# A hybrid decoder layer on one core: output projection with the activations in the array and 512 weight columns moving, and three changes of order

## The chip, the core and the metric

The kernel runs on one core of a Trainium2 chip. A core has TensorE (a 128x128 array, fed by weight loads, writing to PSUM), VectorE, ScalarE, GpSimd and SyncE (SP, which here only issues DMAs), each with its own instruction stream, and 16 DMA engines. The streams meet in semaphores that the program waits on by hand. The metric is the time of one execution in microseconds; lower is better.

## What is computed

One layer for 512 prompt rows and 32 sample rows (8 sequences of 4 tokens), model width 2048, fp32 throughout. Cut to what the change touches:

```python
def _prompt_attention(...):       # 4 blocks of 128 queries
    scores = sum_h w[t,h] * relu(qi[t,h] . ki[s])   # 16 index heads of width 64
    _, idx = lax.top_k(causal scores, 128)          # then sparse attention over idx, 8 heads x 128
def _sample_attention(...):       # the same over 1024 cached keys in 8 pages and the new ones, top 256
    ...
def _combine(x, a, p, ga, gb, w_out, ln_g, ln_b):
    mixed = concat([a * silu(ga), p * silu(gb)])    # 2048 wide
    h = 2 ** 0.25 * x + mixed @ w_out               # w_out 2048 x 2048
    y = (h - mean(h)) * rsqrt(var(h) + 1e-5) * ln_g + ln_b
```

## The kernel before

**Three products.** A large product is done in a split format: each fp32 operand becomes a high part (`actH`, `wH`, format fp32r, one pass) and a low part (`actL`, `wL`), and TensorE adds high x high, low x high and high x low. ScalarE makes `wH` from the raw weights (`high`, L656), GpSimd subtracts it from them to get `wL` (`low`, L634). Weights come through four slots of 8 chunks x 128 columns, 512 KB each (`rawW`, loaded by SP at L426). A slot is loaded anew when its `wL` is done (`stage_ready`), and its high part is made anew when its matmuls are done.

**Projections.** `unit` (L1125) multiplies one slot: weights of 128 columns are in the array, 544 activation columns move in two halves of 272, 48 matmuls a unit, two units a tile (L1138). Tile A are the index queries (8 tiles), C the heads, B the pooling mixer, D the output projection (16 tiles). Since D gives outputs by channel, ScalarE copies each tile to `raw`, TensorE turns it back by token (`rows`, L1647 and L1650), and VectorE adds the residual (L2120, L2124), takes the statistics (L2131) and applies the gain (L2137). The first tile of D (`first_tile`, L1483) is interleaved with the last value pages (L1525), chunk by chunk as `actL` gets ready. After the last tile come variance, square root, and the shift vector of each token, which is turned (L1668) and multiplied with `ln_g` and `ln_b` (`correction`, L1677) before VectorE writes y in pieces (L2185) and SP sends it.

**Index tiles.** For each of the 8 tiles of A, TensorE does half a tile, then index products of the tile before (`products`, L1196), then the other half. ScalarE rectifies each product (`rectify`, L713), VectorE adds it to the scores (`add_head`, L1745). The six products of one tile are numbered 0 to 5. ScalarE copies the projected tile to `raw` (L722) after rectifying product 3, VectorE rotates it (`rotate`, L1714 to L1719) after adding product 3, and `qi_ready` tells TensorE that the products with it may start. For the first tile, all six run at once with a zeroed `raw` as operand, waiting only for `qi_ready` 1.

**Softmax of the first heads.** VectorE picks the top 128 of each prompt row eight at a time (`pick_prompt`, L1789 and L1793), between rotations of keys and queries (`rotated`). The order in the first pair is: 2 picks, gate, 3 picks, rotate, 3 picks, rotate, 1 pick, rotate the second key (`rotated(2, ...)`), 2 picks, keep mask (L1863), softmax (L1876).

**Key pages.** When the prompt heads are done, VectorE turns the sample scores into a mask (L1933), ScalarE sends it to memory (`dropD`, L960), VectorE clears `U` and `qPad`, waits for that DMA, clears `probS` (L1939), places the queries (L1944) and copies key page groups from PSUM (`key_copied`, L1951, even ones; ScalarE does the odd ones after copying a tile of B). TensorE turns the keys (L1438) and multiplies them (L1454: four matmuls with 32 columns of the array each). SP spreads the mask back into `probS` (L507).

**SP's order at the end.** In the last group SP interleaves the loads of the first four units of the second and third D tile with the value pages (`unit`, L523). Then it waits for the last attention output, issues the loads of y (L601, 4 MB, and L602), the broadcast gain, waits for VectorE to clear `gb` (L2113, itself after all of y has landed), sends eight rows to `gb` (L608), and goes on with the weights of D.

Of the kernel before, what the change touches and what calls it, by code (L numbers as in the profile page):

```python
# [32 lines left out]
P = 128  # L33
# [37 lines left out]
TILE_A, TILE_C, TILE_B, TILE_D = 1, 9, 41, 57  # L71
SWAP_I = [*range(8, 16), *range(8), *range(16, 32)]
# [89 lines left out]
def layer_program(nc, x_prompt, x_sample, cache_k, cache_v, cache_kidx, state_pool, page_table,  # L162
# [4 lines left out]
    with ctx:  # L167
# [63 lines left out]
        with ExitStack() as s:  # L231
# [29 lines left out]
            def key_slot(n):  # L261

                if n // 2 % 2:
                    return mixed[:, KC - 2 + n % 2, 0:4 * P]
                return kPT[:, n % 2, :, :].rearrange("p h k -> p (h k)")
        with ExitStack() as s:
            y = sb("y", [P, 5, D], F32, s)
            bn = sb("bn", [P, 5, KC, 6], F32, s)
# [5 lines left out]
        gbc = mixed[:].rearrange("p k t -> p (k t)")[:, 0:D]  # L274
# [5 lines left out]
        bank[OUT], bank[SIDE] = acc[0][:, 0, :], acc[0][:, 1, :]  # L280
        dropD = nc.dram_tensor("dropD", [NS, L], F32, kind="Internal").ap()
# [61 lines left out]
        corr_full = sems("corr_full", 2)  # L343
        y_ready = sems("y_ready", 2)
# [57 lines left out]
        yb = banks.stage(["yp0", "ys0", "yp1", "ys1"], four, 8)  # L402
        tb = banks.stage(["t0", "t1", "t2", "t3"], four)
# [5 lines left out]
        def stand_alone(eng):  # L409


            eng.sem_inc(apart, 1)

# [7 lines left out]
        def _(sp):  # L421
# [100 lines left out]

            def unit(j, last=False, g=None):  # L523
# [4 lines left out]
                if last and tile >= 4:  # L528
                    load_unit(wo_view, 1 - half, (tile - 4) * P, t)
# [42 lines left out]
            def group(g, last):  # L572
# [10 lines left out]
                for m in range(PAGES):  # L583
                    if m % 2 == 0:
# [10 lines left out]
            group(LOOPS, True)  # L595

# [7 lines left out]
            sp.dma_start(gbc, ln_g[0].partition_broadcast(P)).then_inc(ln_in, 16)  # L604
# [4 lines left out]
            with sp.Fori(0, 6) as i:  # L609
                for j in range(2):  # L610
                    load_tile(wo_view, (2 * i + 4 + j) * P, TILE_D + 4 + j, i, 2)
            for t in range(TT + 1):
                n = P if t < TT else NS
                dst = y_prompt[0, t * P:(t + 1) * P, :] if t < TT else y_sample.rearrange("b t d -> (b t) d")
                for half in range(2):
                    cols = slice(1024 * half, 1024 * (half + 1))
                    sp.wait_ge(y_ready[t % 2], (t // 2) * (4 if t % 2 else 2) + (half + 1) * (2 if t % 2 else 1))
# [28 lines left out]
        def _(act):  # L646
# [161 lines left out]
            def heads(i, last):  # L808
# [150 lines left out]
            act.wait_ge(drop_ready, 1)  # L959
            act.dma_start(dropD, scoreS[:]).then_inc(drop_out, 16)  # L960


# [27 lines left out]
            copy_tile(0)  # L990
            for m in range(8):
                key_copied("a", m)
            exps(0)
# [100 lines left out]
            with act.Fori(0, 7) as i:  # L1094
                for j in range(2):
                    high(TILE_D + j + 2, 0, i, 2)
                    src, copied = projected(TILE_D + j, i, 2)
                    act.activation(halves(raw[:, j]), src, ACT.Copy).then_inc(copied, 1)
                    high(TILE_D + j + 2, 1, i, 2)
            for j in range(2):  # L1100
                src, copied = projected(TILE_D + 14 + j)
                act.activation(halves(raw[:, j]), src, ACT.Copy).then_inc(copied, 1)
            act.wait_ge(var_ready, 1)
            act.activation(std[:, 0:2], mv[:, 0:2, 1], ACT.Sqrt).then_inc(std_ready, 1)

            b = tb("t0")
            out_of(b, shiftT[:, 0:2 * P], bank_wait(act, b)[:, 0:2 * P])
            act.wait_ge(var_ready, 3)
            act.activation(std[:, 2:5], mv[:, 2:5, 1], ACT.Sqrt).then_inc(std_ready, 1)
            b = tb("t1")  # L1110
            out_of(b, shiftT[:, 2 * P:T], bank_wait(act, b)[:, 0:T - 2 * P])
# [3 lines left out]
        def _(pe):  # L1115
# [83 lines left out]
            for tile in range(H):  # L1199
# [5 lines left out]

                unit(TILE_A + tile, 0)
                if tile == 0:
# [4 lines left out]
                    products(0, 6)  # L1212
                    continue
# [474 lines left out]
            for n in (2, 3):  # L1688
                take(tb(f"t{n}"))
# [565 lines left out]
```

## Time and profile before

| | us |
|---|---|
| median of 3 runs | 1218.41 (1217.15 to 1219.67) |
| the profiled execution | 1214.59 |
| its span, on which all rows stand | 1212.5 |
| TensorE busy | 1179.9 (97%) |
| weight loads busy | 1087.3 (90%) |
| VectorE busy | 597.2 (49%) |
| ScalarE busy | 359.0 (30%) |
| GpSimd busy | 354.1 (29%) |

The profile is one execution. PE is TensorE's matmuls, PEld its weight loads, DVE VectorE, ACT ScalarE, POOL GpSimd, SPq and ACTq DMA issues of SP and ScalarE. A matmul of fp32 operands appears as two instructions. Busy time of overlapping instructions is counted once, so a busy TensorE is not one at its peak.

### The profile page before, as it was taken

The numbers are of one execution on the slowest core, as the hardware profiler recorded it, in microseconds if no ns is written. First come the engines' busy times: TensorE is split into PE (matmuls) and PEld (weight loads), VectorE is DVE, ScalarE is ACT, GpSimd is POOL, SyncE is SP. The second block draws the span as 40 slices with busy tenths as digits, with TensorE's granted clock in tenths as the row PEclk, the third lists the DMA queues.
The fourth block names the chain that finished last, engine by engine and source line by source line (L and its number), as shares of the span: only waits on it lengthen the run. The fifth ranks groups of instructions, "written<-read, shape, count | busy, mean of one in ns | idle before, by whom it ended". The sixth has DMA issues, their size and how long they took to land.

```text
span 1212.5 us, 26754 instructions
## 1 busy us (share of the span) xinstructions
PE 1179.9 (97%) x10300; PEld 1087.3 (90%) x10300; DVE 597.2 (49%) x1083; ACT 359.0 (30%) x665; POOL 354.1 (29%) x150
## 2 busy tenths in 40 slices
PE   6999999999999999999989999999999999999995
PEld 6888889999999999999987889888889879999992
DVE  3666658874665657451444622623523552323226
ACT  4333333223323323322333322322323342122210
POOL 2432222333333334334311311311321223333310
PEclk9999999999999999999999999999999999999996
DMA  7543143233232223354226857857867656222203
GB/s 250 130 121 80 48 111 89 70 88 89 79 104 82 80 79 98 93 154 129 62 85 196 287 208 245 300 194 250 287 207 248 214 189 219 82 76 86 69 1 147
DMA packets 197975, 170.50 MB, mean 141 GB/s; under 512 B 19890, under 2 KB 178538, under 8 KB 196658
## 3 DMA queue, kind: packets, MB, share of 16 engines
q1 hardware_dynamic: 184458, 160.48, 42.7%
q10 hardware_dynamic: 13424, 8.67, 2.4%
q8 instruction: 72, 1.18, 0.4%
q14 instruction: 21, 0.17, 0.0%
HBM read 159.47 MB, written 9.74 MB: 140 GB/s over the span
## 4 chain that ended last, share of the span: by engine, by line
PE 91%; DVE 6%; issue 1%; DMA 1%; ACT 1%; DVEq 0%; SPq 0%; ACTq 0%
PE acc L1138 67%; PE bank L1438 5%; PE bank L1454 3%; PE acc L1525 3%; PE bank L1196 2%; PE bank L1332 2%; PE bank L1313 2%; DVE scoreP L1793 1%; PE acc L1579 1%; DVE top L1789 1%; PE acc L1483 1%; DMA xnat<-in_x_prompt 1%; PE bank L1248 1%; DVE y L2185 1%; PE bank L1322 1%
## 5 line engine op out<-in xcount | busy, mean ns | idle before, releaser
L634 POOL TENSOR_TENSOR wL<-rawW,wH 128x1024 fp32r<-128x1024 f32 (+1 forms) x146 | 353.9, 2425 | 811.4 <-ACT wH L656 811.4
L1138 PE MATMUL acc<-actH,wH 128*128 128x272 f32 (+1 forms) x2304 | 491.5, 294 | 1.2 <-DVE actL L1707 1.2
L1138 PE MATMUL acc<-actH,wL 128*128 128x272 f32 (+1 forms) x2304 | 476.6, 288 | 0.0
L1138 PE MATMUL acc<-actL,wH 128*128 128x272 f32 (+1 forms) x2304 | 475.0, 288 | 0.0
L1138 PEld LDWEIGHTS acc<-actH,wH 128*128 128x128 f32 (+1 forms) x2304 | 360.1, 188 | 23.9 <-issue 21.9
L1138 PEld LDWEIGHTS acc<-actL,wH 128*128 128x128 f32 (+1 forms) x2304 | 361.4, 188 | 0.0
L1138 PEld LDWEIGHTS acc<-actH,wL 128*128 128x128 f32 (+1 forms) x2304 | 359.1, 188 | 0.0
L656 ACT ACTIVATE wH<-rawW 128x1024 fp32r<-128x1024 f32 (+1 forms) x146 | 153.7, 1054 | 226.2 <-PE acc L1138 210.3
L2120 DVE SCALAR_TENSOR_TENSOR y<-y,bank 128x512 f32 (+1 forms) x16 | 11.0, 688 | 122.3 <-PE bank L1647 120.4
L1438 PE MATMUL bank<-sq,kPage 128*128 128x128 f32 x480 | 65.6, 280 | 4.1 <-DVE kPT L1951 4.0
L1438 PEld LDWEIGHTS bank<-sq,kPage 128*128 128x128 f32 x480 | 52.9, 142 | 14.5 <-issue 9.8
L1951 DVE COPY mixed<-bank 128x512 f32<-128x512 f32 x32 | 22.1, 692 | 86.9 <-PE bank L1438 86.5
L1745 DVE SCALAR_TENSOR_TENSOR scoreP<-relu,wiN,scoreP 128x256 f32<-128x256 f32 (+2 forms) x54 | 45.6, 885 | 33.4 <-ACT relu L713 33.4
L1891 DVE SCALAR_TENSOR_TENSOR mixed<-bank,gate 128x128 f32<-128x128 f32 x32 | 9.3, 292 | 82.2 <-PE bank L1332 82.2
L670 ACT ACTIVATE kPT<-bank 128x512 f32<-128x512 f32 x32 | 19.1, 598 | 92.1 <-PE bank L1438 92.1
L713 ACT ACTIVATE relu<-bank 128x512 f32<-128x512 f32 (+3 forms) x63 | 28.9, 502 | 56.4 <-PE bank L1196 33.0
L670 ACT ACTIVATE mixed<-bank 128x512 f32<-128x512 f32 x32 | 19.1, 598 | 85.6 <-PE bank L1438 79.6
L1830 DVE MAX8 top<-scoreS 32x8 f32<-32x1056 f32 x32 | 39.9, 1247 | 3.1
L1951 DVE COPY kPT<-bank 128x512 f32<-128x512 f32 x32 | 22.1, 691 | 39.0 <-PE bank L1438 38.3
L1525 PE MATMUL acc<-vPage,probST 128*4 128x128 f32 x1024 | 39.5, 273 | 0.0
L1833 DVE MATCH_REPLACE8 scoreS<-top,scoreS 32x1056 f32<-32x1056 f32 x32 | 39.4, 1230 | 0.0
L1525 PEld LDWEIGHTS acc<-vPage,probST 128*4 128x4 f32 x1024 | 26.6, 87 | 13.3 <-issue 1.5
(207 smaller groups left out, 1019.6 us busy)
## 6 DMA issues: line engine op xcount, KB each, us to landing
rawW<-in_w_in SPq DMA_DIRECT2D x112, 512.0 KB, 3.8
vPage<-in_cache_v SPq DMA_DIRECT2D x64, 512.0 KB, 4.8
kPage<-in_cache_k SPq DMA_DIRECT2D x60, 512.0 KB, 4.6
rawW<-in_w_out SPq DMA_DIRECT2D x32, 512.0 KB, 4.1
y<-in_x_prompt SPq DMA_DIRECT2D x4, 1024.0 KB, 9.3
out_y_prompt<-y SPq DMA_DIRECT2D x8, 512.0 KB, 2.8
xnat<-in_x_prompt SPq DMA_DIRECT2D x2, 1024.0 KB, 7.9
xnat<-in_x_prompt ACTq DMA_DIRECT2D x2, 1024.0 KB, 10.9
```

Source lines behind the costliest of these rows:

```text
L634: pool.tensor_tensor(wL[:, slot, :, 0:width], rawW[:, slot, :, 0:width], wH[:, slot, :, 0:width].bitcast(F32), ALU.subtract).then_inc(stag ...
L656: act.activation(wH[:, t.slot, :, 0:width], rawW[:, t.slot, :, 0:width], ACT.Copy).then_inc(high_ready[t.slot], 1)
L670: act.activation(dst, src, ACT.Copy).then_inc(bank_free[b.slot], 1)
L713: act.activation(relu[0:rows, t.slot, 0:n], src[0:rows, 0:n], ACT.Relu).then_inc(relu_full[t.slot], 1)
L1138: last = pe.matmul(acc[t.slot][0:width, e, 0:HT], w[:, u.slot, k, 0:width], a[:, kk, e * HT:(e + 1) * HT], start=(half == 0 and k == 0 and ...
L1438: last = pe.transpose(dst[:, (2 * e + a) * P:(2 * e + a + 1) * P], page[:, h * P:(h + 1) * P], ident)
L1454: last = pe.matmul(bank[st.slot][j * SPAN:(j + 1) * SPAN, pair % 2 * 256:pair % 2 * 256 + 256], qPad[:, x % 2, h * NS:(h + 1) * NS], keys, ...
L1525: return pe.matmul(bank[o.slot][j * SPAN:j * SPAN + NT, a * P:(a + 1) * P], probs, values, start=start and a == 0, stop=stop and a == HALF ...
L1745: dve.scalar_tensor_tensor(sc, relu[:, r.slot, 0:(t + 1) * P], wiN[:, t - 1, ds(h, 1)], sc, ALU.mult, ALU.add).then_inc(bank_free[b.slot], 1)
L1830: own.step(dve.max(top, scores))
L1833: own.step(dve.match_replace(scores, top, scores, PICKED))
L1951: dve.tensor_copy(key_slot(2 * m), bank_wait(dve, b)[:]).then_inc(bank_free[b.slot], 1)
```

## The change

**Output projection.** The activations are in the array (128 tokens at a time) and 512 weight columns move. The outputs come by token, and the copies and turning back go. There are four blocks of 512 output columns, and 8 units of two chunks x 512 columns in each; a unit is one slot of 512 KB. `out_tiles` multiplies a unit with the four prompt tiles, 24 matmuls. The 32 sample rows are done with fp32 weights and activations from the raw slots: after each pair of units, four matmuls of 32 array columns each (`sample_parts`), one for each of the pair's four chunks, accumulate in four groups of 32 partitions; at the end of a block ScalarE copies them out and one matmul with a folding matrix adds the four groups (`folded`). Five PSUM banks are used for each block, in a ring of eight. Because the raw weights are read by TensorE, a slot is loaded anew only when its pair is done (`pair_done`), and the units 4 to 7 of the first block are loaded after the last group's other loads, waiting for pairs 1 and 2. In the last block the first two token tiles are finished ahead of the others. Statistics, gain, square root, correction and output go one token tile at a time, the sample tile third.

**Index tile.** Of the first tile's six products, three run as before, and three after the first half of the next tile.

**Softmax.** `rotated(2, ...)` moves behind the last two picks.

**Key pages.** The mask is made and sent after the last softmax, ahead of the last gating; key page group 0 is copied ahead of the clearing; `probS` is cleared before `qPad` and `U`; the first key groups use the other pair of buffers; ScalarE copies two key groups before the tile of B.

```diff
+WIDE = 4 * P
+BLOCKS = D // WIDE
+PAIRS = (4, 5, 6, 7, 0, 1, 2, 3)
+NORMED = (0, 1, TT, 2, 3)
...
-                if n // 2 % 2:
+                if n // 2 % 2 == 0:
                     return mixed[:, KC - 2 + n % 2, 0:4 * P]
...
+            def load_out_unit(t, n, col, done):
+                if done is None:
+                    sp.wait_ge(stage_ready[t.slot], t.free)
+                else:
+                    sp.wait_ge(pair_done, done)
...
-                    load_unit(wo_view, 1 - half, (tile - 4) * P, t)
+                    load_out_unit(t, j - 8, 0, None if j < 12 else (j - 12) // 2 + 1)
...
-                    if m % 2 == 0:
+                    if m % 2 == 0 and not last:
                         unit(12 + m // 2, last, g)
...
             group(LOOPS, True)
+            for j in range(12, 16):
+                unit(j, True, LOOPS)
...
-            with sp.Fori(0, 6) as i:
-                for j in range(2):
-                    load_tile(wo_view, (2 * i + 4 + j) * P, TILE_D + 4 + j, i, 2)
-            for t in range(TT + 1):
+            with sp.Fori(0, BLOCKS - 1) as i:
+                for n in range(8):
+                    load_out_unit(turn(2 * TILE_D + 8 + n, 4, i, 8), n, (i + 1) * WIDE, 4 * i + (n + 4) // 2 + 1)
...
                     exps(1)
+                    act.wait_ge(drop_ready, 1)
+                    act.dma_start(dropD, scoreS[:]).then_inc(drop_out, 16)
                     probs_turned(1, range(TT))
...
-                    products(0, 6)
+                    products(0, 3)
                     continue
+                if tile == 1:
+                    products_of(0, 3, 6)
                 pe.wait_ge(qi_ready, tile + 1)
...
+            def rows_times(q, t, n, first=False, last=False):
+                for c in range(2):
+                    k = 2 * PAIRS[n % 8] + c
+                    for w, parts in ((wH, (actH, actL)), (wL, (actH,))):
+                        for a in parts:
+                            end = pe.matmul(out_bank(q), a[:, k, t * P:(t + 1) * P], wide(w, n, c),
+                                            start=first and c == 0 and w is wH and a is actH,
+                                            stop=last and c == 1 and w is wL)
...
+            def sample_parts(p):
+                q = 5 * (p // 4) + TT
+                weights_ready(2 * p + 1)
...
+                for j in range(4):
+                    n, c = 2 * p + j // 2, j % 2
+                    end = pe.matmul(out_bank(q)[NS * j:NS * (j + 1), :], mixed[:, 2 * PAIRS[n % 8] + c, NP_:T], wide(rawW, n, c),
+                                    start=p % 4 == 0, stop=p % 4 == 3, skip_group_check=True)
+                end.then_inc(pair_done, 1)
...
+            for n in range(4, 8 * BLOCKS - 4):
+                out_tiles(n)
+                if n % 2:
+                    sample_parts(n // 2)
+                if n % 8 == 0:
+                    folded(n // 8 - 1)
...
+            weights_ready(a)
+            weights_ready(b)
+            sample_parts(4 * BLOCKS - 2)
+            for t in range(2):
+                rows_times(first + t, t, a)
+                rows_times(first + t, t, b)
+            weights_ready(c)
+            rows_times(first, 0, c)
+            weights_ready(d)
+            rows_times(first, 0, d, last=True)
+            sample_parts(4 * BLOCKS - 1)
...
-            picks(1)
+            picks(TOPK_P // ROUND - len(EARLY) - 8)
             rotated(2, kT, 1, 0)
-            picks(TOPK_P // ROUND - len(EARLY) - 9)
...
+            normal(0)
+            normal(1)
+            normal(2)
+            finished(0)
+            normal(3)
+            finished(1)
+            finished(2)
+            normal(4)
+            finished(3)
+            finished(4)
```

`normal` adds the residual, takes statistics, variance and the shift of one token tile; `finished` writes its four output pieces.

## Rows read from the trace of the kernel before

**Rows 1.** The page: chain by engine, one costly group, one DMA issue (median to landing).

```profile
PE 91%; DVE 6%; issue 1%; DMA 1%; ACT 1%; DVEq 0%; SPq 0%; ACTq 0%
...
L634 POOL TENSOR_TENSOR wL<-rawW,wH 128x1024 fp32r<-128x1024 f32 (+1 forms) x146 | 353.9, 2425 | 811.4 <-ACT wH L656 811.4
...
out_y_prompt<-y SPq DMA_DIRECT2D x8, 512.0 KB, 2.8
```

**Rows 2.** TensorE's waits: waiting line, releaser, us in total, times, longest.

```profile
PE bank L1438 <- DVE kPT L1951: 4.0, 1, 4.0
PE bank L1248 <- DVE stat L1876: 2.3, 1, 2.3
...
PE bank L1196 <- DVE scoreP L1745: 0.7, 1, 0.7
```

**Rows 3.** The chain in order of time: start, us, what.

```profile
983.23 3.20 PE acc L1483 x24
...
1168.15 12.03 PE acc L1138 x96
1180.73 6.02 PE acc L1138 x48
```

**Rows 4.** Timeline, TensorE at 889 us: start, us, instruction, idle before.

```profile
889.40 0.19 PEld L1579 LDWEIGHTS acc<-U,wp 128*128 128x128 f32 x1 [0.24 <-issue]
...
889.83 0.19 PEld L1579 LDWEIGHTS acc<-U,wp 128*128 128x128 f32 x1 [0.24 <-issue]
...
890.78 0.64 PE L1454 MATMUL bank<-mixed,qPad 128*32 128x256 f32 x8
...
891.23 0.62 PE L1525 MATMUL acc<-vPage,probST 128*4 128x128 f32 x16
...
891.78 0.98 PE L1438 MATMUL bank<-sq,kPage 128*128 128x128 f32 x7
```

**Rows 5.** Busy time by stretch (PE PEld DVE ACT POOL), then granted clock, DMA.

```profile
637.70:641.10 3.40, 3.34 (x18) 2.20 (x19) 0.70 (x2) 0.60 (x1) 0.00 (x0) 0.50 0.09 22
```

**Rows 6.** Timeline of the first index tile.

```profile
46.22 1.55 PE L1196 MATMUL bank<-kiT,raw 64*128 64x256 f32 x8
...
50.31 0.78 DVE L1714 STREAM_SHUFFLE rot<-raw 128x544 f32<-128x544 f32 x1
...
52.10 2.64 POOL L634 TENSOR_TENSOR wL<-rawW,wH 128x1024 fp32r<-128x1024 f32 x1 [3.92 <-ACT wH L656]
52.52 2.80 DVE L1719 TENSOR_TENSOR raw<-raw,rot 128x544 f32<-128x544 f32 x1
...
56.30 0.92 PE L1196 MATMUL bank<-kiT,raw 64*128 64x256 f32 x4
```

**Rows 7.** Timeline at the first softmax (VectorE) and at the first key pages.

```profile
266.66 0.01 DVE L1714 LOAD_MASK_SELECT rot<-kT  x1 [6.12 <-ACT kT L737]
...
271.71 1.46 DVE L1789 MAX8 top<-scoreP 128x8 f32<-128x256 f32 x3
...
278.47 0.76 DVE L1863 TENSOR_SCALAR keepP<-scoreP 128x1152 bf16<-128x1152 f32 x1
...
636.14 0.94 DVE L1939 MEMSET probS<- 128x1056 f32 x1 [1.73 <-DMA dropD<-scoreS]
...
639.66 1.08 PE L1454 MATMUL bank<-kPT,qPad 128*32 128x256 f32 x8
```

**Rows 8.** Timeline of SP's loads at the projection's start, and ScalarE.

```profile
993.88 1.99 SPq L601 DMA_DIRECT2D y<-in_x_prompt  x4
...
1013.41 20.15 SPq L426 DMA_DIRECT2D rawW<-in_w_out  x7
...
1017.77 1.06 ACT L656 ACTIVATE wH<-rawW 128x1024 fp32r<-128x1024 f32 x1 [5.46 <-DMA rawW<-in_w_out]
```

**Rows 9.** Timeline of VectorE in the tail.

```profile
1190.13 1.03 DVE L2158 BATCH_NORM_AGGREGATE mv<-bn 128x2 f32<-128x96 f32 x2
...
1205.11 2.71 DVE L2185 SCALAR_TENSOR_TENSOR y<-y,stat,bank 128x512 f32<-128x512 f32 x4
```

More of the change, by code:

```diff
@@ L280, in layer_program, with out_bank @@
         bank[OUT], bank[SIDE] = acc[0][:, 0, :], acc[0][:, 1, :]
+        ring = [*(bank[j][:] for j in four), *(acc[j][:, e, :] for j in (1, 0) for e in range(2))]
+        def out_bank(q):
+            return ring[q % len(ring)]
         dropD = nc.dram_tensor("dropD", [NS, L], F32, kind="Internal").ap()
@@ new lines, in bank_clear, with weights_ready @@
+            def bank_clear(q):
+                if q >= len(ring):
+                    pe.wait_ge(out_read, q - len(ring) + 1)
+                elif q in (4, 5):
+                    copied(TILE_D - 1)
+                else:
+                    b = bb({0: "Pt0b", 1: "Pt1b", 2: "S0b", 3: "S1b", 6: "Ob", 7: "OTb"}[q], LOOPS)
+                    assert q >= 6 or b.slot == four[q]
+                    pe.wait_ge(bank_free[b.slot], b.read)
+            def weights_ready(n):
+                u = out_unit(n)
+                pe.wait_ge(stage_ready[u.slot], u.read)
@@ L1491, in _, with folded @@
+            def folded(b):
+                pe.wait_ge(gb_clear, 1)
+                pe.wait_ge(part_copied, b + 1)
+                pe.matmul(out_bank(5 * b + TT)[0:NS, :], fold[:], raw[:, b % 2, 0:WIDE], start=True, stop=True
+                          ).then_inc(fold_full, 1)
             copied(TILE_C + 31)
@@ L1636, in _ @@
                 group(g, g == LOOPS)
-            for name in ("Ob", "OTb"):
-                b = bb(name, LOOPS)
-                pe.wait_ge(bank_free[b.slot], b.read)
-            def rows(j, i):
-                copied(TILE_D + j, i, 2)
-                b = yb(f"yp{j}", i)
-                dst = take(b)
-                for t in range(TT):
-                    last = pe.transpose(dst[:, t * P:(t + 1) * P], raw[:, j, t * P:(t + 1) * P], ident)
-                full(b, last)
-                b = yb(f"ys{j}", i)
-                full(b, pe.transpose(take(b)[0:NS, 0:P], raw[:, j, NP_:T], ident))
@@ L1652, in _ @@
-            with pe.Fori(0, 7) as i:
-                for j in range(2):
-                    unit(TILE_D + j + 1, 0, i, 2)
-                    rows(j, i)
-                    unit(TILE_D + j + 1, 1, i, 2)
-            unit(TILE_D + KC - 1, 0)
-            rows(0, 7)
-            unit(TILE_D + KC - 1, 1)
-            rows(1, 7)
-            def shift_turned(name, tiles, ready):
-                b = tb(name)
-                dst = take(b)
-                pe.wait_ge(var_ready, ready)
-                for n, t in enumerate(tiles):
-                    m = P if t < TT else NS
-                    last = pe.transpose(dst[:, n * P:n * P + m], shift[0:m, t, :], ident[0:m, 0:m])
-                full(b, last)
@@ L1694, in _ @@
+            shift_turned(2)
+            rows_times(first + 3, 3, d, last=True)
+            correction(2)
+            for at in (3, 4):
+                shift_turned(at)
+                correction(at)
         @block.vector
@@ L1982, in _ @@
             queries(0)
-            for m in range(5):
+            for m in range(1, 5):
                 key_copied("a", m)
@@ L2170, in _ @@
[L2170 to L2186 removed]
+            reads = 0
```

309 lines of the change are left out of this document (171 added, 138 removed).

## The prediction

> **What bounds the kernel now.** The chain of work that ended last comes first: 91% of it is TensorE [rows 1], so time is won where TensorE's stream gets shorter or stops waiting. TensorE's waits come next [rows 2]: 4.0 us at the first key pages, 2.3 us at the first softmax, 0.7 us at the first index tile. The chain in order of time prices the output projection [rows 3]: one of its 16 tiles takes 12.58 us (1180.73 less 1168.15), of which 96 matmuls of 272 columns take 12.03 us, 125.3 ns each, and the turning back 0.55 us. It runs from 983.23 to 1186.75, 203.5 us: 96 matmuls of the first tile (12.0), 2.9 us of value pages between them, then the other tiles. From there to the end of the span, 25.8 us belong to the tail. All sums below are made against the span of 1212.5 us. The profiled execution took 1214.59 us, 3.8 us less than the median of the three runs shown (1218.41), and I add the change of the span to that median.
>
> **The projection's matmuls.** 1536 matmuls of 272 columns and their 80 transposes go; 4 blocks x 16 chunks x 4 token tiles x 3 products = 768 matmuls of 512 columns come. The trace has no such matmul in this format. Nearest is the fp32 one of 512 columns, which makes two passes: its weight loads start 0.43 us apart [rows 4] for 1024 column steps, 0.42 ns a column and some 4 ns over the 213.3 ns that 512 columns take at 2.4 GHz and one pass. So 217.6 ns as the lower end. From the 272-column row, 12 ns over its 113.3 ns, a fixed surcharge gives 225.3 ns, and a surcharge by column 235.9 ns. I take 217.6: loading 128 weight columns is what a short matmul may fail to hide, and under 512 columns it has twice the time. 768 x 0.2176 = 167.1 us (173.0 or 181.2 by the others).
>
> The Trainium skill ("TensorE: Matmul & The Clock Gate", Back-to-back issue gap) gives N/2.4 + 2.5 ns, 215.8 ns here; for 272 columns it gives 115.8 where the row has 125.3, so it is short by 9.5 ns there. By it the sum is 1.4 us lower. The same section gives about 131 ns for 512 columns in a sustained stream of loads and matmuls; that is a rival below.
>
> **The 32 sample rows.** They become 16 groups of four fp32 matmuls, 32 columns of the array each, 512 moving. Whether four run at once is shown by the key products: eight passes of 256 columns take 0.45 us (890.78 to 891.23), where one after another they would take 1.7 [rows 4]. So a group is two passes, 2 x 0.43 + 0.03. Entering and leaving the narrow tiling costs 0.1 each way: the last wide pass starts at 890.26 and should end at 890.68, the next starts at 890.78; the narrow ones should end at 891.66, the next starts at 891.78. 1.09 us a group, 17.4 in all. Four folding matmuls at the same price are 4.3, two correction groups that now lie ahead of the last matmul 2.2, three small transposes 0.4. The value pages keep their 2.9. Together 194.3 us: without waits the last projection matmul ends at 983.2 + 194.3 = 1177.5, not 1186.75.
>
> **The tail.** Now each token tile is normed while others are still multiplied. Call X the end of the first tile's last product. After X TensorE has the last sample group, 10 batches of 6 matmuls (13.1), one fold and two corrections: 17.7 us with the transposes, so X = 1159.8. VectorE has five tiles: residual, statistics and gain are passes over 512 columns, 0.68 each like an output piece [rows 9]; an aggregate takes 0.45 (0.51 with four times the entries [rows 9]); four small operations with their waits 0.6. So 3.1 us each, and 2.7 us for four output pieces [rows 9]: 29 us, with 1.3 us of waits for TensorE ahead. VectorE sets the end: X + 30.3, and 2.9 us for the last 512 KB. The half tile that is last now lands 2.8 us after its issue [rows 1]. That gives 1193.0, a gain of 19.5 us.
>
> **What the new order of loads costs.** The sample products read the raw weights, so a slot is free only when its pair is done. In the steady state a pair lasts 11.5 us (48 x 0.2176 + 1.09), and a unit needs 4.36 us from issue to ScalarE [rows 8], 1.05 us there and 2.4 us on GpSimd [rows 1], the second of a pair 10 us in all: hidden. In two places it isn't. First, at the end sample group 14 and four batches last 6.3 us, but units 30 and 31 are ready 7.7 and 10.1 us after their slots come free: X moves by 2.5 us. Second, SP now waits for pair 2 before loading units 6 and 7, and the loads of y stand behind that. Pair 2 is done at 983.2 + 4 units x 5.22 + two sample groups 2.2 + 2.9 = 1009.2, where the y loads were issued at 993.88 before. From there SP waited for y to land and for VectorE to clear gb, sent eight gb rows, and issued the next weights at 1013.41, 19.5 us after y [rows 8]. Now 1 MB of weights (units 6 and 7) goes ahead of y and delays it by some 3 us, 0.8 of them before y is issued: unit 8 is issued at 1010.0 + 19.5 + 2.2 = 1031.7 and ready 4.36 + 1.05 + 2.4 = 7.8 us later, at 1039.5. TensorE wants it two pairs after 1009.2, at 1032.3: a wait of 7.2 us, between 5 and 9 by how much of the 3 us shows and how fast 2 KB pieces land. ScalarE and GpSimd have nothing else there; it is SP's queue that is late, and behind TensorE's wait stands the whole rest.
>
> **The clock.** After the 4.0 us wait TensorE's granted clock is 0.50, 1.2 GHz, for 3.4 us of work [rows 5]: 1.7 us lost. The 7.2 us wait I price the same, or 3.4 if the clock stays low twice as long: 8.9 with the wait.
>
> **The index tile.** Products 3 to 5 of the first tile move behind the first half of the next one, which saves 0.7 us [rows 2]. But ScalarE copies the projected tile only after the rectification of product 3, and VectorE rotates it only after adding product 3; the products of the next tile wait for that rotation. Before, the rotation took 50.31 to 55.32, its last operation 2.8 us, beside GpSimd's subtraction of 52.10 to 54.74, and TensorE came at 56.30 [rows 6]. Now three products (about 1.5 us from 46.22) and 6.2 us of unit put product 3 at 53.9; 2.0 us later it is added (product, rectify 0.4, add 0.65), the last rotation operation starts at 58.1, beside GpSimd's next subtraction (ScalarE's high part moved behind product 5, so 57.8 to 60.2), and ends at 60.9. TensorE resumes at 61.1: 4.8 us late, 2.7 if the two don't meet. With the clock 6.5 us lost.
>
> **Softmax.** Two picks of 3.4 us each (271.71 to 278.47) move into VectorE's 6.1 us of idling before the key rotation [rows 7]. The rotation ends about 1 us later, at 272.6, TensorE needs it at about 277.8; the masks start some 5 us sooner than they did and the 2.3 us wait goes. Nothing else there is late for another 3 us.
>
> **Key pages.** The mask goes to memory early, in time that VectorE and ScalarE idle, so the round trip of 1.7 us is gone and key page 0 is copied before the clearing [rows 7]. VectorE: copy 0.7, clear 0.94, clear 0.5, queries 0.12 after the transposes at 633.3 give 635.8, so the first key products start at 635.9, not 639.66, and the half clock that still lay on the 1.4 us after 639.66 goes too, 0.7 us: 4.4 us. The cover of the mask DMAs shrinks to nothing by the first masking at 641.5; if they come late, 1 to 1.5 us return.
>
> **Sum**: -19.5 (projection and tail), +2.5 (last units), +8.9 (first block's end), +6.5 (index tile), -2.3 (softmax), -4.4 (key pages) = **-8.3 us**: span 1204.2, a median of **1210.1 us**.
>
> **Rivals.** (a) The surcharge of the 272-column row is fixed: 225.3 ns, +5.9 us, 1216.0. For it: same format; against: the fp32 row. (b) It goes by column: 235.9 ns, +14.1 us, 1224.3, slower than before. It decides from 228.4 ns up (8.3 us / 768 more). For it: 0.461 ns a column holds over thousands of matmuls; against: 0.421 in the fp32 row. (c) The four sample matmuls run one after another: 3.45 us, +41 us in all, 1251; against it stand the key products [rows 4]. (d) One of the two waits I foresee isn't there, because y lands sooner or the rotation isn't held: 1201.2 or 1203.6; for it, that I read them from the order of code and not from a trace. (e) The waits are longer, the clock stays low twice as long, or loads meet elsewhere: +6, 1216. (f) By the rule just named, 131 ns: the array would take 3.9 columns a ns where rows show 2.2 and 2.4; -66 us, 1144 [rows 3, 4].
>
> **Chances.** Forecast 0.50, (a) 0.13, (b) 0.10, (c) 0.02, (d) 0.15, (e) 0.09, (f) 0.01. Forecast alone: 1205 to 1215. The range reaches to (d) and near (b), 1201 to 1222. A measurement can tell about 0.2%, 2.4 us. Faster: 0.46 of the forecast, (d), (f) and parts of (a) and (e), 0.70; same 0.12; slower 0.18.
>
> **What would show it.** The spacing of the 512-column matmuls (217 ns); TensorE waiting near 55 us for the rotation, over 4 us; no wait at the first softmax, under 1 us at the key pages; a wait of 5 to 9 us 49 us after the projection begins, its weights issued late by SP; and VectorE busy through the tail of about 33 us from X. Any other spacing, or sample groups above 1.2 us, makes it wrong.

## The result, and the profile after

| | before | after |
|---|---|---|
| median of 20 runs | 1217.77 us (1214.03 to 1219.67) | 1221.03 us (1218.16 to 1223.06) |
| ratio to before | 1 | 1.0025, 95% interval 1.0018 to 1.0032 |
| profiled execution | 1214.59 us | 1221.41 us |
| its span, mean granted clock | 1212.5 us | 1219.2 us, 0.988 |

The changed kernel is 3 us slower; the forecast was 8.3 us faster. The profiled run of before lies 3.8 us under the median that the forecast used, so the spans (+6.7 us) overstate the difference. Most of that lies in the start: the profile of before has no stretch at half clock in its first 60 us, where every other profile here has one of 3.4 or 6.8 us between 20 and 30 us.

TensorE's waits after the change (engine, what waits, what it waited for: us in total, times, longest), to be read beside [rows 2]:

```profile
PE acc L1552 <- POOL wL L671: 6.8, 3, 4.7
PE bank L1227 <- DMA sq<-const_square: 6.6, 1, 6.6
PE bank L1253 <- DVE raw L1828: 5.3, 1, 5.3
PE acc L1765 <- ACT shiftT L1151: 4.7, 1, 4.7
```

The 2.3 us at the softmax and the 4.0 us at the key pages are gone (1.0 us is left at the latter). In their place stand 5.3 us at the index tile (L1253) and 4.7 us at the first block's end (L1552), both foreseen. The 6.6 us (L1227) belong to the start-up, and the 4.7 us at L1765 to the tail, where VectorE's pieces come last.

The new large matmuls, in the chain (start us, us, what), to be read against [rows 3]:

```profile
1056.62 0.99 PE bank L1580 x8
1057.61 4.39 PE acc L1552 x18
...
1063.38 4.18 PE acc L1552 x18
```

18 matmuls of 512 columns in 4.18 us are **232 ns** each at full clock. The forecast had 217.6. The median of each stretch of 10 us of the projection lies between 231 and 235, whatever the other engines do meanwhile. A sample group (L1580) takes 0.99 us itself, and the wide matmuls beside it take longer, as the timeline shows (start us, busy us, engine, line, out<-in, shapes, count):

```profile
1080.65 0.39 PE L1552 MATMUL bank<-wH,actL 128*128 128x512 f32 x1
1080.88 0.40 PE L1552 MATMUL bank<-wL,actH 128*128 128x512 f32 x1
1081.21 1.07 PE L1580 MATMUL bank<-rawW,mixed 128*32 128x512 f32 x8
1082.21 0.50 PE L1552 MATMUL acc<-wH,actH 128*128 128x512 f32 x1
1082.54 0.39 PE L1552 MATMUL acc<-wH,actL 128*128 128x512 f32 x1
```

0.23 us from one wide start to the next, but 0.33 before the group and 0.33 behind it: with both, a group costs 1.20 us.

The index tile, same view, and what SP did before unit 8 (chain):

```profile
60.35 5.41 POOL L671 TENSOR_TENSOR wL<-rawW,wH 128x1024 fp32r<-128x1024 f32 x2 [10.48 <-ACT wH L693]
60.81 2.75 DVE L1828 TENSOR_TENSOR raw<-raw,rot 128x544 f32<-128x544 f32 x1
63.62 1.65 PE L1253 MATMUL bank<-kiT,raw 64*128 64x256 f32 x4 [5.26 <-DVE raw L1828]
```

```profile
1015.73 14.84 DMA y<-in_x_sample
...
1030.80 0.50 DVE gb L2228
1031.31 0.27 SPq L645
...
1034.10 4.09 DMA rawW<-in_w_out
...
1039.34 2.36 POOL wL L671
...
1041.75 6.73 PE acc L1552 x18
```

18 matmuls that took 4.18 us above take 6.73 here, 2.5 us more: the clock. It shows in the windows (span of the window, its us, busy us of each engine, TensorE first, granted clock, DMA share, GB/s), one at each of the two waits:

```profile
60.33:67.16 6.83, 3.54 (x12) 2.47 (x13) 6.80 (x6) 1.49 (x3) 5.41 (x2) 0.50 0.65 168
1039.96:1046.79 6.83, 5.04 (x12) 3.98 (x13) 2.25 (x2) 3.23 (x4) 6.83 (x4) 0.50 0.29 106
```

Both stretches of 6.83 us began while TensorE still waited, 3.3 us before the first wait ended (63.62) and 1.8 before the second (1041.75). So only 3.5 and 5.0 us of them were work at half clock, which costs half of it: about 1.8 and 2.5 us, not 3.4 each. Before, the one such stretch ahead of the tail lasted 3.4 us and was all work [rows 5], since it began where the wait ended. In the second stretch the matmuls start 427 ns apart (nine spacings in 3.84 us):

```profile
1042.34 0.63 PE L1552 MATMUL acc<-wH,actL 128*128 128x512 f32 x1
...
1046.18 0.63 PE L1552 MATMUL acc<-wH,actL 128*128 128x512 f32 x1
```

That is 512 columns at 1.2 GHz with nothing on top, where at full clock 18.7 ns come on top.

**Where the time went, by the two traces.** The chain reaches the same unit of the heads 8.9 us later (259.81 before, 268.73 after). Of these 2.9 us are the start-up, which the change doesn't touch: the first projection begins 1.5 us later (23.09 against 21.59; the constants' DMA landed later in this execution), and its first 144 matmuls take 1.4 us more, for a stretch at half clock that the profile of before hasn't (chain, before and after):

```profile
21.59 18.21 PE acc L1138 x144
...
23.09 19.61 PE acc L1195 x144
```

So the index tile costs 6.0 us by the traces. Past the first softmax it is 6.4 us late, at the key pages 2.5, at the start of the projection 2.1 (985.25 against 983.16). From there to the end of the span it takes 233.95 us, before 229.3.

### The profile page after: what moved, and what is told of

It is laid out like the page before. It is cut to its first block, busy times and chain, and to the rows that moved or that the text cites. A ratio compares the mean times of both kernels' runs of the same rounds, so it can differ in the third digit from the quotient of the medians.

```text
span 1219.2 us, 24992 instructions
## 1 busy us (share of the span) xinstructions
PE 1185.1 (97%) x9588; PEld 1037.8 (85%) x9588; DVE 599.1 (49%) x1016; ACT 353.9 (29%) x660; POOL 353.8 (29%) x150
## 4 chain that ended last, share of the span: by engine, by line
PE 89%; DVE 5%; DMA 3%; issue 1%; ACT 1%; SPq 1%; POOL 0%; POOLq 0%; DVEq 0%
PE acc L1195 53%; PE bank L1552 7%; PE acc L1552 5%; PE bank L1500 5%; PE bank L1516 3%; PE acc L1625 3%; PE bank L1253 2%; PE bank L1375 2%; PE bank L1394 2%; PE acc L1679 1%; DVE scoreP L1902 1%; DMA y<-in_x_sample 1%; DVE top L1898 1%; DMA xnat<-in_x_prompt 1%; PE bank L1310 1%
## 5 line engine op out<-in xcount | busy, mean ns | idle before, releaser
L1195 PE MATMUL acc<-actH,wH 128*128 128x272 f32 (+1 forms) x1824 | 392.1, 296 | 1.2 <-DVE actL L1816 1.2
L1195 PE MATMUL acc<-actH,wL 128*128 128x272 f32 (+1 forms) x1824 | 378.0, 289 | 0.0
L1195 PE MATMUL acc<-actL,wH 128*128 128x272 f32 (+1 forms) x1824 | 376.8, 288 | 0.0
L1195 PEld LDWEIGHTS acc<-actH,wH 128*128 128x128 f32 (+1 forms) x1824 | 285.8, 188 | 24.3 <-issue 22.4
L1195 PEld LDWEIGHTS acc<-actL,wH 128*128 128x128 f32 (+1 forms) x1824 | 286.7, 188 | 0.0
L1195 PEld LDWEIGHTS acc<-actH,wL 128*128 128x128 f32 (+1 forms) x1824 | 284.8, 188 | 0.0
L1552 PE MATMUL bank<-wH,actH 128*128 128x512 f32 x160 | 65.0, 406 | 0.0
L1552 PE MATMUL bank<-wL,actH 128*128 128x512 f32 x160 | 63.0, 394 | 0.0
L1552 PE MATMUL bank<-wH,actL 128*128 128x512 f32 x160 | 62.9, 393 | 0.0
L1552 PE MATMUL acc<-wH,actH 128*128 128x512 f32 x96 | 40.0, 417 | 6.8 <-POOL wL L671 6.8
L1552 PEld LDWEIGHTS bank<-wH,actH 128*128 128x128 f32 x160 | 30.0, 188 | 16.1 <-issue 9.7
```

Of the source, the lines that this page charges most:

```text
L1195: last = pe.matmul(acc[t.slot][0:width, e, 0:HT], w[:, u.slot, k, 0:width], a[:, kk, e * HT:(e + 1) * HT], start=(half == 0 and k == 0 and ...
L1552: end = pe.matmul(out_bank(q), a[:, k, t * P:(t + 1) * P], wide(w, n, c), start=first and c == 0 and w is wH and a is actH, stop=last and ...
```

## The experiments

Ratios are to the kernel before, timed beside each experiment; its medians were 1217.5 to 1218.2 us. 0.1% is 1.2 us. The runs p1 to p4 are one execution each and are read for the spacing of matmuls, not for their time.

**e1: the index tile alone undone.**

```diff
-                    products(0, 3)
+                    products(0, 6)
                     continue
-                if tile == 1:
-                    products_of(0, 3, 6)
```

> The changed kernel with one part undone: the six products of the first index tile are issued together again, none of them behind the half unit of the next tile. Theory (the moved products hold up the rotation, as the prediction said, and the clock falls behind it): the wait of 5.3 us near 63.5 us goes, about 0.7 us comes back near 46 us, the granted clock no longer falls to 0.50 for 6.8 us, of which half is lost: 1221.0 - 5.3 + 0.7 - 3.4 = 1213 us. Rival (the clock falls there anyway, or the time is taken back at a later wait for VectorE or GpSimd): only the wait goes, 1216 us, or nothing, 1221 us.

Measured: 1213.46 us, ratio 0.9970 (0.9960 to 0.9981). That is 7.6 us under the changed kernel by the medians and 6.7 by the ratios. The wait for the rotation is gone, a wait of 0.5 us for VectorE's addition is back, and the clock stays full from 40 to 62 us.

The theory holds, but its 3.4 us for the clock were too many. By the trace the move costs the wait of 5.3 us and 1.8 us of half clock, less the 0.5 us: 6.6 us. In e1's profiled execution the first block's end was cheaper as well: from the first to the last product of the projection it takes 215.1 us, the changed kernel 216.9. That the sum came out at 1213 us is luck in part.

**e2: weights of units 8 to 11 issued ahead of the gb rows.**

```diff
             sp.dma_start(gbc[:], ln_g[0].partition_broadcast(P)).then_inc(ln_in, 16)
+            for n in range(4):
+                load_out_unit(turn(2 * TILE_D + 8 + n, 4), n, WIDE, (n + 4) // 2 + 1)
             sp.wait_ge(gb_clear, 1)
```

> The changed kernel with one part moved: SP issues the weights of units 8 to 11 of the output projection ahead of the eight gb rows, not behind them. Theory (SP's queue is what is late at the end of the first block): the wait of 4.7 us near 1041.6 us goes and with it the half clock of 6.8 us, of which 3.4 us are lost: 1221.0 - 8.1 = 1213 us. Rival (the transfers or GpSimd's subtraction are what is late, or the clock falls there for another reason): 1216 us or more, with a wait of over 2 us left at that place.

Measured: 1214.48 us, ratio 0.9972 (0.9961 to 0.9983), 6.5 us under the changed kernel. Of the three waits for `wL` (waits of TensorE) the one of 4.7 us is gone, and no half clock lies there:

```profile
PE acc L1556 <- POOL wL L675: 2.1, 2, 1.4
```

And its chain, where the 4.7 us stood:

```profile
1027.15 11.32 PE bank L1556 x48
...
1039.47 4.42 PE acc L1556 x18
```

So SP's place in line was the cause, not the transfer itself or GpSimd. From the first to the last product the projection takes 209.8 us, 7.1 us less than in the changed kernel, as the wait (4.7) and the clock (2.5) add up to; the 8.1 us of the theory counted the clock too high. The times show 6.5 us.

**e3: the orders at the softmax and the key pages alone, on the kernel before.**

```diff
-            picks(1)
+            picks(TOPK_P // ROUND - len(EARLY) - 8)
             rotated(2, kT, 1, 0)
-            picks(TOPK_P // ROUND - len(EARLY) - 9)
...
+                    act.wait_ge(drop_ready, 1)
+                    act.dma_start(dropD, scoreS[:]).then_inc(drop_out, 16)
                     probs_turned(1, range(TT))
...
+            key_copied("a", 0)
             dve.wait_ge(drop_out, 16)
```

> The kernel before with the new orders at the softmax and at the key pages alone; index tile and output projection as before. Theory (these two parts give what the prediction said, 2.3 and 4.4 us, and nothing takes it back): 1217.8 - 6.7 = 1211 us. Rival (the gain is taken back, as the trace of the changed kernel hints: its key pages begin 2.5 us later than before though the index tile costs 8 us, so 5.5 us of gain rather than 6.7, less if the start is to blame): 1213 to 1216 us.

Measured: 1210.74 us, ratio 0.9945 (0.9932 to 0.9958): 6.7 to 6.9 us gained, where the prediction had 2.3 + 4.4. What stays of TensorE's waits there:

```profile
PE bank L1453 <- DVE qPad L1948: 1.0, 1, 1.0
```

The rival falls: nothing takes this gain back. Nor did it in the changed kernel: its key pages begin only 2.5 us late because 2.9 of start-up and 6.0 of the index tile stand against 6.4 of gain.

**e4: the new projection and tail alone** (the changed kernel with e1's diff, and e3's reversed).

> The kernel before with the new output projection and tail alone; index tile, softmax and key pages as before. Theory (the parts add: 1221.0, less 7.6 for the index tile, plus 6.9 for the orders taken away): 1220.3 us, 2.7 us above the kernel before, because 768 matmuls at 232 to 235 ns and sample groups of 1.2 us use up the gain and the late unit 8 costs 6.5 us. By the prediction on record it was to be 8.1 us below it (1209.7). A rival in which the parts don't add lies between the two.

Measured: 1221.84 us, ratio 1.0029 (1.0019 to 1.0039), 3.5 us above the kernel before. The parts add: orders -6.7, projection +3.5, index tile +6.7 make +3.5 us, where the whole change measures +3.0. The part from which the forecast drew its gain (-8.1 us with its wait and last units) is the part that is 11.6 us off.

**p1: what a matmul costs by its width.**

```diff
-                            end = pe.matmul(out_bank(q), a[:, k, t * P:(t + 1) * P], wide(w, n, c),
+                            for lo, hi in (((0, 512),), ((0, 256), (256, 512)), ((0, 384), (384, 512)),
+                                           ((0, 128), (128, 256), (256, 384), (384, 512)))[t]:
+                                end = pe.matmul(out_bank(q)[:, lo:hi], a[:, k, t * P:(t + 1) * P], wide(w, n, c)[:, lo:hi],
```

> The changed kernel with the 512 moving columns cut in pieces, another cut for each token tile of the output projection: tile 0 keeps 512, tile 1 takes 2 x 256, tile 2 takes 384 + 128, tile 3 takes 4 x 128; the same array contents and data. It prices a matmul by its width. Theory L (a surcharge that grows with the columns, on the line through 125.3 ns at 272 and 232 ns at 512: 4.5 ns + 0.4444 ns a column): 256 columns 118.2 ns, 384 columns 175.1 ns. Theory F (512 columns carry something that narrower ones don't, such as the weight load or the full bank; below that a fixed 12 ns over the columns at 2.4 GHz): 256 columns 118.7 ns, 384 columns 172.0 ns, 128 columns 65 ns or, if bound by the weight load, more. The two differ at 384 by 3 ns over 24 or more matmuls of each kind.

Measured, in the timeline (each line one product of a token tile, in its pieces):

```profile
1107.36 0.40 PE L1554 MATMUL acc<-wH,actH 128*128 128x256 f32 x2
...
1108.80 0.40 PE L1554 MATMUL acc<-wH,actH 128*128 128x384 f32 x2
1109.03 0.45 PE L1554 MATMUL acc<-wH,actL 128*128 128x384 f32 x2
...
1110.46 0.61 PE L1554 MATMUL bank<-wH,actH 128*128 128x128 f32 x4
...
1112.69 0.61 PE L1554 MATMUL bank<-wL,actH 128*128 128x128 f32 x4
```

256 columns: 1.44 us for 12, 120 ns (119.3 as the mean of all). 128 columns: 2.23 us for 20, 111.5 ns, twice what they take to move. I read this as the bound of the weight load, though no run changed the load at this width. The pair 384 + 128: 1.43 us for five, 286 ns; less 111.5 for the short one, 174.5 ns. The first pair of a tile gives 384 columns without a difference, since the short one starts 174 to 180 ns behind it. So what comes on top of the columns at 2.4 GHz is 12.6 ns at 256, 12.0 at 272, 14.5 at 384, 18.7 at 512. Neither rule is exact: it is not fixed, and it doesn't go wholly by column. Theory L's line (118.2 and 175.1) is within 1.2 ns of both, F's (172.0) lies under every one of these. A matmul is no faster per column when wide: 0.466 ns at 256, 0.461 at 272, 0.453 at 512. Twice the width bought 2%.

**p2: the same 512 columns in other kinds of matmul.**

```diff
+                            left, right = a[:, k, t * P:(t + 1) * P], wide(w, n, c)
+                            if t == 2:
+                                left, right = w[:, out_unit(n).slot, c, :], a[:, k, 0:512]
+                            if t == 3:
+                                left, right = left.bitcast(F32), right.bitcast(F32)
...
+                                            start=t == 1 or first and c == 0 and w is wH and a is actH,
```

> The changed kernel with another kind of matmul for each token tile of the output projection, 512 moving columns each; the products of tiles 1 to 3 are not those of the reference. Tile 0 as it is; tile 1 without accumulation (each matmul starts its bank anew); tile 2 with the weights in the array and the activations moving; tile 3 with the same bytes read as plain fp32. Theory S (reading and multiplying this split-precision format costs about 0.45 ns a column whatever moves and wherever it adds): 232 ns for tiles 0 to 2; tile 3 two passes of 215 ns, 430 ns, as the fp32 row of the trace of before. Theory A (the sum in the full bank costs it): tile 1 near 217 ns. Theory M (it is the moving weights, by their place in memory): tile 2 near 217 ns. Theory L (any full matmul loads 128 columns beside 512 moving and loses some): tile 3 would be at 446 ns or more.

Measured (timeline; tile 1 begins at 1111.15, tile 2 at 1112.54, tile 3 at 1113.93):

```profile
1111.15 0.40 PE L1557 MATMUL acc<-wH,actH 128*128 128x512 f32 x1
...
1112.54 0.40 PE L1557 MATMUL acc<-actH,wH 128*128 128x512 f32 x1
...
1113.93 1.02 PE L1557 MATMUL bank<-wH,actH 128*128 128x512 f32 x2
1114.79 1.02 PE L1557 MATMUL bank<-wH,actL 128*128 128x512 f32 x2
```

Tiles 1 and 2: 1.39 us for six, 232 ns each. Tile 3: 0.86 us a matmul, in two passes of 429 ns. So neither the sum in the bank (A) nor the choice of what moves (M) makes the 232 ns, and a full plain fp32 pass isn't at 446 ns (against L). S holds for tiles 0 to 2. Its number for tile 3 was wrong by a factor of two: I had written two passes of 215 ns, 430 in all, and it is two passes of 429, 858 in all. 429 ns for one pass of 512 columns is two steps a column, 1024 steps, only 2.4 ns over what they take at 2.4 GHz. What this format has on top of its columns, a pass at half the column rate doesn't have; nor has this format itself at half clock (427 ns, above).

**p3: a smaller array filling, and bf16.**

```diff
+                            if t == 1 ...:
+                                left, dst = left[:, 0:64], dst[0:64, :]
+                            if t == 2:
+                                left, right = left[0:64, :], right[0:64, :]
+                            if t == 3:
+                                left = left.bitcast(BF16)[:, 1::2]
+                                right = right.bitcast(BF16)[:, 1::2]
```

> The changed kernel with another array filling for each token tile of the output projection, 512 moving columns each; the products of tiles 1 to 3 are not those of the reference. Tile 0 as it is (232 ns); tile 1 with 64 columns in the array for all but its first and last matmul; tile 2 with 64 rows; tile 3 with the upper halves of the same words read as bf16, in the same places. Theory W (the load of the next 128 columns takes time from the moving stream): tile 1 loses half the surcharge, 223 to 225 ns, tile 2 stays at 232 ns. Theory S (the split-precision format moves slower than 2.4 columns a ns): tiles 1 and 2 at 232 ns, tile 3 at 216 to 218 ns. Theory C (TensorE shares its reading with something else, whatever the format): all four at 232 ns.

Measured, in the timeline:

```profile
1106.46 0.40 PE L1560 MATMUL bank<-wH,actH 128*64 128x512 f32 x1
...
1107.61 0.40 PE L1560 MATMUL bank<-wL,actH 128*64 128x512 f32 x1
1107.94 0.50 PE L1560 MATMUL acc<-wH,actH 64*128 64x512 f32 x1
1108.27 0.39 PE L1560 MATMUL acc<-wH,actL 64*128 64x512 f32 x1
...
1109.78 0.39 PE L1560 MATMUL acc<-wH,actL 128*128 128x512 bf16 x1
...
1110.68 0.39 PE L1560 MATMUL acc<-wL,actH 128*128 128x512 bf16 x1
```

64 columns in the array: 1.15 us for five, 230 ns; 64 rows: 235 ns (the median); so W (223 to 225 ns) falls: halving the weight load gives back 2 ns at most. bf16 takes 225 ns (0.90 us for four), between S's 217 and C's 232: part of the surcharge, 12 of 18.7 ns, is there for bf16 too, read with a stride of two elements, so S isn't the whole of it either. What the array or its reading does in those nanoseconds stays open.

**e7: both repairs, e1 and e2 together.**

> The changed kernel with both repairs: the index tile's six products together, and units 8 to 11 issued ahead of the gb rows. Theory (the two losses are independent, 7.6 and 6.5 us by the two runs before this one, and nothing else takes them back): 1221.0 - 14.1 = 1207 us. Rival (a wait behind one of them takes part of it back): 1210 to 1213 us.

Measured: 1207.77 us, ratio 0.9913 (0.9899 to 0.9928); 13.3 us under the changed kernel by the medians. The two losses are independent as far as this tells (14.1 were expected). Unit 8 is now ready 0.35 us after TensorE wants it; its weights, issued at 1017.97 us, share the queues with y and take 8.87 us (chain):

```profile
1017.97 8.87 DMA rawW<-in_w_out
```

**p4: cheaper sample groups.**

```diff
-                for j in range(4):
+                for j in range(4) if p % 4 != 1 else range(3, 4):
...
+                    cols = NS if p % 4 == 2 else WIDE
```

> The changed kernel with both repairs and cheaper sample groups: of each block's four groups the second has one of its four matmuls (512 columns), the third has all four with 32 columns instead of 512; the sample rows of the first output are not those of the reference. Theory N (the four narrow matmuls run at once, two passes of 0.43 us, and entering and leaving the narrow tiling costs 0.1 us each way on the wide matmuls beside it, so 1.20 us a group and not the 1.09 of the prediction): the second group also takes 1.0 us and 0.2, the third 0.2 for the tiling plus about 0.15, so 0.85 us less than a full one. Rival (c) of the prediction (the four run one after another): the second group takes a quarter of a full one. Rival E (the 0.2 us belongs to the long passes): it is absent around the third group.

Measured, in the timeline (the second group of a block, then a third):

```profile
1105.85 1.04 PE L1580 MATMUL acc<-rawW,mixed 128*32 128x512 f32 x2
1106.83 0.50 PE L1551 MATMUL bank<-wH,actH 128*128 128x512 f32 x1
1107.16 0.39 PE L1551 MATMUL bank<-wH,actL 128*128 128x512 f32 x1
...
1118.14 0.27 PE L1580 MATMUL acc<-rawW,mixed 128*32 128x32 f32 x8
1118.34 0.50 PE L1551 MATMUL bank<-wH,actH 128*128 128x512 f32 x1
1118.68 0.39 PE L1551 MATMUL bank<-wH,actL 128*128 128x512 f32 x1
```

One matmul of the four takes 0.98 us where all four take 0.99: they run at once, and rival (c) is out. The short group takes 0.20 us, and 0.1 us still lies on each side of it (0.34 us behind it from 1118.34 to 1118.68). So a visit to the narrow tiling puts 0.2 us on the matmuls beside it whatever is done in it, as theory N had it.

**e8 and e10: the tail.** e8 swaps `finished(2)` and `normal(4)` on VectorE; e10 also moves TensorE's last transpose:

```diff
-            for at in (3, 4):
-                shift_turned(at)
-                correction(at)
+            shift_turned(3)
+            shift_turned(4)
+            correction(3)
+            correction(4)
```

> The changed kernel with both repairs and one swap in VectorE's tail: the statistics of the fourth token tile (the last product to come, at 1202.3 us in the changed kernel) go ahead of the four output pieces of the sample rows. In the changed kernel VectorE waits 1.6 us for TensorE before those pieces, takes them in 2.7 us, then the statistics in 2.8 us, then waits 1.7 us for the last shift. Theory (the order on VectorE sets the end): the statistics begin 3.6 us sooner, the wait of 1.7 us goes, the pieces that follow run one after another: 1.7 us of wait and about 1 of the 1.6 us before it come back, 1207.8 - 2.7 = 1205 us. Rival (TensorE's corrections, at half clock by then, become what VectorE waits for): 1207 to 1208 us.

> The run e8_tail_order with TensorE's order changed too: the last shift is transposed before the corrections of the fourth output tile, not behind them. Theory (in e8 the last transpose stood in TensorE's queue behind corrections that wait for VectorE's pieces, so VectorE then waited 2.1 us for the last corrections): that wait of 2.1 us goes, and the pieces of the last three tiles follow one another: about 2.6 us from X to the end less than in e7_both, 1207.9 - 2.6 = 1205.3 us. Rival (corrections at half clock keep VectorE waiting in any order): 1207 to 1208 us, with waits of VectorE for them left in the trace.

> The run e7_both again, beside e10_tail_both, since the two differ by less than a run of before does from call to call: 1207.8 us. If it comes out over 1209 or under 1206.5 us, differences of 1 us between calls mean nothing.

e8 measured 1208.02 us, ratio 0.9918 (0.9905 to 0.9932): no gain that the times show, the theory fell. VectorE's waits for corrections shrank only from 4.9 to 3.6 us, since one engine's wait had become the other's. In e8 the statistics come sooner, but TensorE's last transpose stood behind corrections that wait for VectorE's pieces (timeline of TensorE):

```profile
1193.15 3.95 PE L1764 MATMUL acc<-gb,shiftT 2*128 2x512 f32 x8 [2.35 <-DVE y L2281]
1197.04 0.47 PE L1753 MATMUL bank<-sq,shift 128*128 128x128 f32 x1
1197.88 2.14 PE L1764 MATMUL acc<-gb,shiftT 2*128 2x512 f32 x8 [0.37 <-ACT shiftT L1155]
```

e10 measured 1206.14 us, ratio 0.9906 (0.9891 to 0.9921); e7 again, timed beside it, 1209.17 us, ratio 0.9928 (0.9914 to 0.9941). Their runs don't overlap (1205.99 to 1207.09 against 1207.93 to 1209.75), so the two orders together are worth 3 us by the medians. The traces say 2.5: from the end of the last large product to VectorE's last piece the changed kernel and both runs of e7 take 13.95 us, e8 13.3 and e10 11.45. TensorE's order was not changed alone, so how much of it is its own stays open. VectorE's last pieces now follow one another (waits of 0.16 and 0.22 us), though TensorE is at half clock (timeline of VectorE):

```profile
1192.19 2.70 DVE L2282 SCALAR_TENSOR_TENSOR y<-y,stat,acc 32x512 f32<-32x512 f32 x4
1195.05 2.75 DVE L2282 SCALAR_TENSOR_TENSOR y<-y,stat,acc 128x512 f32<-128x512 f32 x4 [0.16 <-PE acc L1764]
1198.02 2.72 DVE L2282 SCALAR_TENSOR_TENSOR y<-y,stat,acc 128x512 f32<-128x512 f32 x4 [0.22 <-PE acc L1764]
```

e7 again came out 1.4 us above its first run, over the mark I had set: between sets of runs made apart, single microseconds say nothing, and e8 against e7 is to be read so. e10, the changed kernel with three small repairs of order, is the fastest version here, 11.4 us under the kernel before and 4.6 under e3's 1210.74 (timed apart).

## Why the prediction was wrong

**The matmul's price, the step that failed.** I took 217.6 ns from the fp32 row [rows 4], reading 4 ns over the columns out of it, and it is 232 ns: 768 x 14.4 = 11.1 us, against the projection's miss of 11.6; the other terms below nearly cancel. Even the 4 ns don't stand in the row: half of its 0.43 us is 215 ns, under 2 over the columns. The fp32 row was a neighbour by width only; its array moves a column in two steps, and p2 shows that such a pass lacks the surcharge. The row of the same format [rows 3] was the nearer one, and its surcharge by column, rival (b), gave 235.9 ns. I gave (b) 0.10 and set its deciding point at 228.4 ns; the measured price lies past it. The reason that I gave for the low end, that a short matmul may fail to hide the weight load, is refuted: by p1 a matmul with its own load fits in 111.5 ns, so the load fits under the 125.3 of a 272-column one, and p3 shows that half of it buys 2 ns at most. The Trainium skill ("TensorE: Matmul & The Clock Gate", Back-to-back issue gap) gives 215.8 ns by its formula and about 131 ns for a stream of loads and matmuls; this stream shows 232.

**The sample groups**: 1.20 us, not 1.09. The 0.1 us each way was right; it lies on the wide matmuls on both sides. What I had too small is the group itself, 0.99 us and not 2 x 0.43 + 0.03 = 0.89. With four folds and two corrections it is 22 x 0.1 = 2.2 us more.

**The first block's end**: right in place and cause (e2). Unit 8's weights were issued 48.85 us after the projection began, forecast 48.5, and it was ready at 56.5, forecast 56.3. The wait was 4.7 and not 7.2 us because TensorE itself came 2.7 us later, 192 slower matmuls being 2.8 us. The clock loss was 2.5 us, not 1.7: together 7.3 by the trace, 6.5 by e2's time, forecast 8.9.

**The last units**: 1.4 and 0.7 us of waits, forecast 2.5. **The tail**: from the end of the first tile's last product (1182.6) to the end of the span 36.6 us, forecast 33.2. I had VectorE as its bound with 1.3 us of waits; it waited 6.1 us in six places, since TensorE's part took 19.7 us (to 1202.3) and not 17.7, and two orders cross there (e8, e10). At half clock from 1207.2 four corrections take 2.1 us where they had taken 1.0.

**Up to the first tile's end** these terms make 708 x 14.4 ns + 18 x 0.1 - 1.6 (first block's end) - 0.5 (last units) = 9.9 us more than forecast, and the trace has 9.4.

**The index tile**: forecast +6.5, 6.7 to 7.6 by e1, 6.0 by the traces less the start-up. The rotation's last operation began 0.45 us behind a GpSimd subtraction and took 2.75 us, as forecast; the wait was 5.3 us (4.8 forecast) and the clock's loss 1.8 (1.7). That the clock came out so close is luck: the low stretch was twice as long as the one I priced it by, and half of it fell into the wait. **Softmax and key pages**: 6.7 forecast, 6.7 to 6.9 measured (e3).

So every other step was within 3.4 us, and the sum had the wrong sign through the one price that stands 768 times in it. Had I taken 232 ns, the same sum would have been +2.8 us, and with the groups +5.0; measured +3.0. That a rival (b) with nearly this price stood in the list doesn't save the forecast, which gave it 0.10.

## What to carry to other kernels

A price that is multiplied by hundreds needs a row of the same format and column rate, not of the same width; where two rows disagree, the forecast should carry both with their weight, and here the wider matmul was only 2% cheaper per column. A loss that hangs on order alone (a weight load behind eight small DMAs, three products behind half a unit) costs its wait and then the work that runs at the lower clock behind it (only the part of the low stretch that outlasts the wait), and is found by asking whose queue the instruction stands in. When one of two engines that wait for each other is reordered, reorder the other with it.

## What the runs showed of the hardware that I had not expected

- A matmul of 512 columns in the split format takes 232 ns at full clock, 18.7 ns over its columns, in either role of the operands, with or without accumulation, and within 2 ns with half of the array's columns; at half clock 427 ns, nothing over its columns; in bf16 with stride two 225 ns; in plain fp32 two passes of 429 ns, 2.4 ns over their steps each.
- At 128 columns a matmul with its own weight load takes 111.5 ns, where its columns take 53.
- Going from 128 columns to 32-column tiles and back, or from 128 to 64 rows and back (p3), puts 0.1 us on the matmul before, each time (0.33 us between starts where 0.23 is usual).
- In waits of 4.7 and 5.3 us the granted clock fell to 0.50 before the wait ended (by 1.8 and 3.3 us) and stayed there for 6.8 us; in one of 3.8 us (e1, at the first block's end) and one of 4.0 us [rows 5] it fell within 0.4 us of the end, for 3.4 us. The softmax wait of 2.3 us [rows 2] had no half clock behind it.
